# The first layer of the compression MLP, moved from small fp32 products to the unit ring, with the token windows stationary

## The reference, cut to what matters

```python
def _compress(z, pe, w1, w2):          # z: (B, T, G, D), T = 256, G = 2; D = 192 for keys, 128 for values
    ch = z.reshape(B, T // CMP_STRIDE, CMP_STRIDE, G, D)          # stride 16, block 32 tokens
    nc = T // CMP_STRIDE - r + 1                                  # 15 blocks
    blk = jnp.concatenate([ch[:, i:i + nc] for i in range(r)], axis=2)
    blk = blk + pe[None, None, :, None, :]
    flat = blk.transpose(0, 1, 3, 2, 4).reshape(B, nc, G, CMP_BLOCK * D)
    return jax.nn.silu(flat @ w1) @ w2                            # w1: (32 * D, 256)
```

## Time and profile before

| | before |
|---|---|
| median of three executions | 2555.05 us |
| the profiled execution, its own time | 2549.53 us |
| its span, first to last instruction | 2547.3 us |
| mean granted TensorE clock | 0.986 |
| TensorE busy | 2486.6 us (98%) |
| TensorE weight loads busy | 2435.2 us (96%) |
| VectorE busy | 1444.2 us (57%) |
| ScalarE busy | 1162.5 us (46%) |
| GpSimd busy | 125.4 us (5%) |
| HBM read | 408.33 MB, 161 GB/s over the span |

### The profile page before, as it was taken

The page is one execution under the profiler, slowest core; times in us unless marked ns, Lnnn a source line. Parts: engine busy times, 40 slices in busy tenths (PEclk is TensorE's granted clock), DMA queues, the critical chain, the costliest instruction groups (busy, mean ns, idle before and its releaser), DMA issues.

```text
span 2547.3 us, 51023 instructions
## 1 busy us (share of the span) xinstructions
PE 2486.6 (98%) x19836; PEld 2435.2 (96%) x19836; DVE 1444.2 (57%) x2171; ACT 1162.5 (46%) x1645; POOL 125.4 (5%) x161
## 2 busy tenths in 40 slices
PE   7999999999999999999999999999998989999987
PEld 7999999899999999999999999999998979999987
DVE  6666335765565555455554556555555456755645
ACT  5555224443454444434443445554454445655542
POOL 3000210000001000000000001000000100000001
PEclk9999989999999999999999999999999989999999
DMA  6446664446666666666676657646554635645543
GB/s 251 164 164 163 181 164 112 117 133 182 178 184 183 182 182 189 190 182 181 182 197 180 183 163 212 169 136 164 139 162 109 166 100 150 166 132 145 152 132 99
DMA packets 750335, 415.20 MB, mean 163 GB/s; under 512 B 44432, under 2 KB 738704, under 8 KB 750224
## 3 DMA queue, kind: packets, MB, share of 16 engines
q1 hardware_dynamic: 746448, 400.78, 56.3%
q0 software_dynamic: 2944, 10.49, 1.3%
q10 hardware_dynamic: 832, 2.36, 0.2%
HBM read 408.33 MB, written 2.10 MB: 161 GB/s over the span
## 4 chain that ended last, share of the span: by engine, by line
PE 90%; DVE 4%; ACT 2%; issue 2%; DMA 1%; POOL 0%; ACTq 0%; DVEq 0%; SPq 0%; POOLq 0%
PE ps_unit L248 26%; PE ps_unit L250 26%; PE ps_unit L249 26%; DVE w_lo L235 1%; PE ps_score L565 1%; ACT w_hi L228 1%; PE ps_score L988 1%; POOL work L2479 0%; PE ps_out L833 0%; PE ps_norm L833 0%; DVE work L351 0%; DVE work L2410 0%; PE ps_score L812 0%; PE ps_norm L1344 0%; PE ps_turn L812 0%
## 5 line engine op out<-in xcount | busy, mean ns | idle before, releaser
L235 DVE TENSOR_TENSOR w_lo<-raw,w_hi 128x1024 fp32r<-128x1024 f32 (+1 forms) x756 | 885.6, 1213 | 242.1 <-ACT w_hi L228 241.2
L228 ACT ACTIVATE w_hi<-raw 128x1024 fp32r<-128x1024 f32 (+1 forms) x756 | 764.1, 1042 | 420.8 <-PE ps_unit L250 418.8
L248 PE MATMUL ps_unit<-b_hi,w_hi 128*128 128x256 f32 (+1 forms) x3184 | 911.2, 286 | 6.0 <-DVE w_lo L235 6.0
L250 PE MATMUL ps_unit<-b_hi,w_lo 128*128 128x256 f32 (+1 forms) x3184 | 906.1, 285 | 0.0
L249 PE MATMUL ps_unit<-b_lo,w_hi 128*128 128x256 f32 (+1 forms) x3184 | 904.4, 284 | 0.0
L248 PE MATMUL ps_unit<-a_hi,w_hi 128*128 128x256 f32 (+1 forms) x2768 | 795.3, 287 | 5.3 <-DVE w_lo L235 3.1
L249 PE MATMUL ps_unit<-a_lo,w_hi 128*128 128x256 f32 (+1 forms) x2768 | 787.5, 284 | 0.0
L250 PE MATMUL ps_unit<-a_hi,w_lo 128*128 128x256 f32 (+1 forms) x2768 | 787.2, 284 | 0.0
L248 PEld LDWEIGHTS ps_unit<-b_hi,w_hi 128*128 128x128 f32 x3184 | 602.0, 189 | 11.9 <-issue 5.1
L250 PEld LDWEIGHTS ps_unit<-b_hi,w_lo 128*128 128x128 f32 x3184 | 602.5, 189 | 0.0
L249 PEld LDWEIGHTS ps_unit<-b_lo,w_hi 128*128 128x128 f32 x3184 | 599.8, 188 | 0.7
(11 more groups left out here) (368 smaller groups left out, 1723.7 us busy)
## 6 DMA issues: line engine op xcount, KB each, us to landing
raw<-in_attn_w_in SPq DMA_DIRECT2D x96, 512.0 KB, 4.9
raw<-in_gla_w_in SPq DMA_DIRECT2D x96, 512.0 KB, 4.4
raw<-in_w_in SPq DMA_DIRECT2D x88, 512.0 KB, 4.8
raw<-in_w_ffn_gate SPq DMA_DIRECT2D x88, 512.0 KB, 4.6
raw<-in_w_ffn_up SPq DMA_DIRECT2D x88, 512.0 KB, 4.7
raw<-in_w_fox SPq DMA_DIRECT2D x64, 512.0 KB, 4.1
raw<-in_w_ffn_down SPq DMA_DIRECT2D x64, 512.0 KB, 4.7
raw<-in_w_out SPq DMA_DIRECT2D x32, 512.0 KB, 4.5
```

Of the source, the lines that this page charges most:

```text
L228: act.activation(hi[:, b % 4, 0:size], raw[:, b % 8, 0:size], ACT.Copy)\
L235: dve.tensor_tensor(lo[:, b % 4, 0:size], raw[:, b % 8, 0:size], hi[:, b % 4, 0:size], ALU.subtract).then_inc(lo_ready, 1)
L248: pe.matmul(dst, wh, xh[:, k0 + k, 0:N], start=start and k == 0, stop=False)
L250: mm = pe.matmul(dst, wl, xh[:, k0 + k, 0:N], start=False, stop=stop and k == kb - 1)
```

## The change

The first layer's operands change sides and its weights enter the ring. The 80 tiles of w1 (32 of 128 key rows, 16 that hold the 64 tail rows of two neighbouring positions one above the other, 32 of values) are laid out on the host as `w_cmp`, 20 blocks of four 128x256 tiles, in the order `CMP_ORDER`. Ten new units `cmp_unit` of two such blocks stand behind slots 5 to 14; they pass raw, `w_hi` and `w_lo` like all others. The windows are split too, into 30 high and 30 low columns side by side (`window_hi` on ScalarE, `window_lo` on VectorE, in slots 3, 4 and 9), and stand stationary, up to 128 columns of them (60 of the tile, and the next tile's first). Each tile takes two products of 256 moving columns, one with `w_hi` and one with `w_lo`, into PSUM rows 0 to 59 of `psS[1]`, where the rows of high and low windows stay apart. At U_NQ ScalarE copies the 60x512 result (`chs`), and four fp32 products with the constant K_SUM add the two halves and turn it; one Silu of 128x120 follows. The tails' windows are now made by VectorE in eight small instructions (`cmp_tails`), for which slot 2's evacuation is written twice. GpSimd's weight loads and its tail windows are gone.

```diff
-U_NQ = U_NKV + 15
+U_NQ = U_NKV + 25
+CMP_ORDER = [*range(32), *range(33, 48), 32, 48, *range(50, 80), 49]
...
+        def cmp_tails(dve):
+            dve.wait_ge(evacuated, nkv(2) + 1)
...
+                        ins = dve.tensor_tensor(cpt[p, 8 * half:8 * half + 8, g * NB_C:(g + 1) * NB_C],
+                                                win, pe_b, ALU.add)
+            ins.then_inc(cp_tails, 1)
...
+        def window_hi(act, m):
+            act.wait_ge(*((cp_ready, 1), (cp_tails, 1), (cp_ready, 2))[m])
+            act.activation(window(0, m), cw[m][0], ACT.Copy).then_inc(cw_hi, 1)
+        def window_lo(dve, m):
+            dve.wait_ge(cw_hi, m + 1)
+            dve.tensor_tensor(window(1, m), cw[m][0], window(0, m), ALU.subtract).then_inc(cw_lo, 1)
+        def cmp_unit(pe, c):
+            U = nkv(5 + c) + 1
+            for h in range(2):
+                b = 2 * U + h
+                pe.wait_ge(lo_ready, b + 1)
+                for t in range(4):
...
+                    rows = min(P, 60 * (n - j))
+                    dst = psS[1][0:rows, T * (m == 2):T * (m == 2) + T]
+                    x = x[:, 60 * j:60 * j + rows]
+                    pe.matmul(dst, x, hi[:, b % 4, T * t:T * (t + 1)], start=q in (0, 48), stop=False)
+                    mm = pe.matmul(dst, x, lo[:, b % 4, T * t:T * (t + 1)], start=False, stop=q in (47, 79))
+                mm.then_inc(block_done, 1)
-        def cmp_piece(pe, m):
...
-            for jj in range(4):
-                for h in range(2):
-                    mm = pe.matmul(cmp_banks[2 * (src == 2) + h][:, 0:30],
-                                   w1s[0:p, m % 3, jj, h * P:(h + 1) * P], x[0:p, j + jj, :],
...
                     if slot in (9, 10, 14):
-                        nsa_turn_v(pe, (9, 10, 14).index(slot), U - 1)
-                    if slot >= 4:
-                        for _ in range(2):
...
-            for m in pieces:
-                cmp_piece(pe, m)
+                        nsa_turn_v(pe, (9, 10, 14).index(slot), nkv(slot - 1))
+                    if slot >= 5:
+                        cmp_unit(pe, slot - 5)
...
+                    pe.wait_ge(cm_h, 1)
+                    for m in range(4):
+                        mm = pe.matmul(psS[0][:, 30 * m:30 * m + 30], chs[:, P * m:P * m + P],
+                                       con[0:60, K_SUM:K_SUM + 30], start=True, stop=True)
...
-                    for v in range(2):
-                        for h in range(2):
-                            ins = act.activation(hsl[:, v, h, :], cmp_banks[2 * v + h][:, 0:30], ACT.Silu)
+                    act.wait_ge(cm_t, 1)
+                    ins = act.activation(hsl.rearrange("p v h n -> p (v h n)"), psS[0][:, 0:120], ACT.Silu)
...
-            for m in range(3, len(CPIECES)):
-                cmp_load(pool, m)
```

More of the change, by code:

```diff
@@ L521, in program @@
         nk_vt, nk_v = sem("nk_vt"), sem("nk_v")
-        cw_full = [sem(f"cw_full{n}") for n in range(3)]
-        cw_used, cp_ready = sem("cw_used"), sem("cp_ready")
+        cp_ready, cp_tails, cw_hi, cw_lo = (sem("cp_ready"), sem("cp_tails"), sem("cw_hi"), sem("cw_lo"))
+        cm_sum, cm_h, cm_t = sem("cm_sum"), sem("cm_h"), sem("cm_t")
         cm_hs, cm_kc, cm_kcr, cm_sq, cm_ms, cm_rs = (
@@ L526, in program @@
         w2_full = sem("w2_full")
[L529 to L543, removed]
+        w_cmp = a["w_cmp"]
@@ new lines, in nkv @@
+        def nkv(slot):
+            return U_NKV + slot + max(0, slot - 5)
+        def cmp_tails(dve):
+            dve.wait_ge(evacuated, nkv(2) + 1)
+            for x in range(2):
+                p = slice(64 * x, 64 * x + 64)
+                for g in range(NSA_G):
+                    for half in range(2):
+                        win = kt2[p, g, 16 * half:16 * half + 240]\
+                            .rearrange("p (n m x) -> p m n x", m=8, x=2)[:, :, :, x]
+                        pe_b = VB[p, V_PET + 8 * half:V_PET + 8 * half + 8].unsqueeze(2)\
+                            .broadcast_to([64, 8, NB_C])
+                        ins = dve.tensor_tensor(cpt[p, 8 * half:8 * half + 8, g * NB_C:(g + 1) * NB_C],
+                                                win, pe_b, ALU.add)
+            ins.then_inc(cp_tails, 1)
@@ L1746, in _ @@
                 fox(h)
[L1747 to L1754, removed]
+            for slot in range(15):
+                U, st = nkv(slot), slot // 5
+                ck, cv = ((C_KC, C_VC), (C_KS, C_VS), (C_KW, C_VW))[st]
+                if slot % 5 == 2:
+                    load_tails(sp, U, 0, 0, ck)
+                else:
+                    load_unit(sp, U, 0, 0, w_in, (ck, ck + NSA_DK, 0, cv, cv + P)[slot % 5])
+                if slot >= 5:
+                    for h in range(2):
+                        load_block(sp, U + 1, h, 0, 0, w_cmp[2 * (slot - 5) + h]
+                                   .rearrange("p (k m) -> p k m", m=P))
             with sp.Fori(0, 4) as i:
@@ L1845, in _ @@
                 fox(h)
-            pieces = iter(range(len(CPIECES)))
             for st in range(3):
                 for s in range(5):
-                    U, slot = U_NKV + 5 * st + s, 5 * st + s
+                    slot = 5 * st + s
+                    U = nkv(slot)
                     mm_unit(pe, U, 0, 0, AH, AL)
@@ L2057, in _ @@
             for slot in range(15):
[L2058 to L2059 removed]
+                U = nkv(slot)
+                if slot >= 5:
+                    split_hi(act, U + 1, 0, 0)
+                split_hi(act, nkv(slot + 1), 0, 0, tails=1 if slot in (1, 6, 11) else None)
                 if slot == 0:
@@ L2065, in _ @@
                     fox_out_hi(act, FOX_H - 1)
+                if slot == 9:
+                    act.wait_ge(block_done, 2 * U)
+                if slot in (3, 4, 9):
+                    window_hi(act, (3, 4, 9).index(slot))
                 if slot in (7, 12):
@@ L2081, in pair @@
                 n = 0 if first else 2 * (i - 1)
+                if first:
+                    act.wait_ge(block_done, 2 * U_NQ)
+                    act.activation(chs, psS[1][0:60, :], ACT.Copy).then_inc(cm_h, 1)
                 split_hi(act, U_NQ + 1, 4, i)
@@ L2091, in pair @@
                     nsa_exp(act, n)
-                split_hi(act, U_NQ + 2, 4, i, tails=i + 1)
+                split_hi(act, U_NQ + 2, 4, i, tails=i + 2)
                 if first:
@@ L2267, in _ @@
             for slot in range(15):
-                U, g, k = U_NKV + slot, slot % 5, slot // 5
-                split_lo(dve, U + 1, 0, 0)
+                U, g, k = nkv(slot), slot % 5, slot // 5
+                nxt, more = nkv(slot + 1), 1 + (slot >= 5)
+                if slot >= 5:
+                    split_lo(dve, U + 1, 0, 0)
+                    lo_block(dve, 2 * nxt)
+                else:
+                    split_lo(dve, nxt, 0, 0)
                 if slot == 1:
```

80 lines of the change are left out of this document (46 added, 34 removed).

## The result

| | before | after |
|---|---|---|
| median | 2555.72 us (4 executions, 2552.21 to 2556.85) | 2509.19 us (4 executions, 2506.33 to 2512.49) |
| the profiled execution, its own time | 2549.53 us | 2511.03 us |
| its span | 2547.3 us | 2509.2 us |
| mean granted TensorE clock | 0.986 | 0.992 |

The ratio of the changed kernel's time to the other's is 0.9828, 95% interval 0.9812 to 0.9843: 1.7% faster, 46.5 us by the medians. The forecast was 2514.5 us with a range of 2507 to 2532.

What follows compares the result with a forecast made beforehand. TensorE, busy 98% of the span, was taken to bound the kernel. Terms -46.9 - 14.1 + 19.1 + 0.9 + 0.5 = -40.5 us took 2555.05 to 2514.5 us, range 2507 to 2532.

Steps and rivals of the forecast that it cites:

- The old products, 46.9 us: Eleven groups of 30-column fp32 products on TensorE, 0.22 us a product, would go: 46.9 us removed.
- The clock, 14.1 us: Eleven units between and behind the old products would return to 5.72 us each at full clock: 14.1 us removed.
- The new products, 0.119 us each, 19.1 us: 160 fp32r products of 256 columns on TensorE, in ten new units, priced like existing units' products: 19.1 us added.
- The fp32-price rival: New products' window loads cost 0.22 us each, 35 us instead of 19, giving 2530.5 us; chance 0.06.
- The last rival: A small product costs by moving columns: old ones worth 5 us, the change adds 20, giving 2570 us; chance 0.01.
- The four small products, 0.9 us: Four fp32 products of 30 columns at U_NQ, 0.22 us each: 0.9 us added on TensorE.
- VectorE late behind slots 8 and 13, 0.5 us: Behind the norms there, the next unit waits for VectorE's evacuation of the shared PSUM bank, twice 0.3: 0.5 us added.
- Loading, ScalarE, GpSimd at nothing: In the shortened stage, SP's loads at 237 GB/s, ScalarE at 50 of 88 us and GpSimd's work add no time.
- The starving ring: w1's loads on SP's queue come too slowly, a slot takes 12.65 us, giving 2565 us; chance 0.02.
- The rival of the low clock: TensorE's clock stays down for another reason, such as heavy loading: +21 us, giving 2535 us; chance 0.06.
- The stage: From the end of slot 4's unit to the end of U_NQ's: 88 us forecast, against 128.63 before.
- The step that was off: The 40.5 us saving, derived from a profiled execution of 2549.5 us, was subtracted from the median of 2555.05 us.

Runs made afterwards that it cites:

- wide: The kernel before with each small product's 30 moving columns repeated eight times, 240 in all, same weight loads; 2570.61 us.
- same sides: The changed kernel with w1's split blocks stationary again and 60 or 30 window columns moving, in fp32r, first layer's result not formed; 2538.49 us.
- rows512: The changed kernel with w1's blocks laid out so that each load is made of 512 B rows instead of 4 KB ones; 2509.74 us.
- the other comparison: The kernel before and the changed kernel, both unedited, timed again with more rounds: medians 2553.85 and 2508.71 us, ratio 0.9827.
- few old: The kernel before with 52 of its 192 small products left, loads and order kept, most of the first layer's sum left out; 2521.63 us.
- dve_plus1: The changed kernel with one more VectorE instruction of 128x1024 behind the fourth split of each of slots 5 to 14; 2508.72 us.
- dve_plus2: The changed kernel with two more VectorE instructions of 128x1024 in each of slots 5 to 14; 2515.46 us.

## Why the prediction was right, and where it was off

- **The old products, 46.9 us**: right for the profiled execution. In the longer course the groups take 49.4 and 50.5 us, since they run partly at the low clock too ("the groups themselves hardly slow" did not hold there).
- **The clock, 14.1 us**: the mechanism was right and shown from two sides (wide and same sides). The size was that of one of two courses; in the other the stage is 7.1 us longer.
- **The new products, 0.119 us each, 19.1 us**: measured 0.1175, and 19.6 us for the ten groups with the slower first product behind each norm or transpose. The fp32-price rival (stationary cuts at every 60th column) is out. The last rival, by which a small product costs by its moving columns, is out as well, and same sides shows it on its own ground: 30 and 60 columns cost the same 0.11 us. The table for products by themselves in the Trainium skill's page "TensorE: Matmul & The Clock Gate", section "Back-to-back issue gap", gives no price for this stream, and what the section says of streams, that loads and products both set the spacing, is what the trace agrees with.
- **The four small products, 0.9 us**: 1.01 us.
- **VectorE late behind slots 8 and 13, 0.5 us**: 0.2 us at slot 10's unit, none at U_NQ. The walk was right in kind: the row of instructions without a gap ends at 303.18.
- **Loading, ScalarE, GpSimd at nothing**: right. 255 GB/s with a share of 0.94, against 237 estimated, and no wait of TensorE for a load. The estimate was low because the stage moves 22.1 MB now, not "the same bytes", 20.8. The starving ring is out, and rows512 shows that there is room.
- **The rival of the low clock**, 21 us, is out: the clock is 1.00 in the whole stage. Its 1.6 us a unit are the loss of one slow unit (7.3 - 5.7); by the mean over the eleven in the earlier trace rows, 7.00 - 5.72 = 1.28, it would have cost some 17 us and stood at the edge of the range, not outside it.
- **The stage**: 88 us forecast (87.2 by the prediction's own terms), 86.66 measured, against a profile it was to be 41.4 us shorter without the four products, and was 42.0.
- **The step that was off** is the last: "It is 5.5 under the median, which is what is predicted: 2555.05 - 40.5". It carried the saving of an execution of the shorter course over to a median that stands near the longer one: three of the four executions behind the 2555.72 us took 2555.05 to 2556.85, as the two profiled ones of the longer course did (2555.61 and 2556.56). In the other comparison, of nine, the median was 2553.85. The 5.5 us between the profiled execution and the median, noted in the prediction, were largely this stage, which differs by 7.1 us between the courses, and so part of what the change could remove. With the longer course the sum would have been -47.6 us and the forecast 2507.4, with both equally often 2511.0; measured were 2509.2. It wasn't cancelling errors that kept the forecast near: each of its five terms stands within 1 us of what the first profiles before and after show.

Outside the stage the spans differ by little: 2417.5 to 2418.8 us in the four profiles before, 2418.4 and 2422.5 in the two after, of which 1.0 are the four products. The rest appears without the change too: wide and few old, both made from the kernel before, stand at 2421.0 and 2422.6. One piece of it shows in all three long ones, at the first hand-over to the second block's attention. TensorE idles there in every kernel, and the granted clock of the 20 us around it is 1.00 in the first profile before and the second after, and 0.83 in the first profile after and in wide and few old. Why it falls in some executions isn't settled.

No experiment with the whole computation in it was faster than the changed kernel: dve_plus1's 2508.72 us and rows512's 2509.74 are single times inside its 2506.33 to 2512.49.

## What to carry to other kernels

A product with few moving columns was paid twice here: by its 128 stationary columns, and by the clock of whatever stood behind it. When one operand is thin (here 30 rows against 256), make the thin one stationary and stream the wide one. A gap of several us between the profiled execution and the median can be a part of the kernel that runs in more than one way: look for it in several profiles before a saving is carried from one to the other, above all where the granted clock is under 1.00. And before taking work from the bounding engine, ask what that work covers: here the next 13.6 us would have brought 3.5.

## What the runs showed of the hardware that I had not expected

- The clock loss behind small products made the same kernel's stage 128.5 to 128.6 us long in two profiled executions and 135.7 to 135.8 in two others, with nothing between in these four.
- A TensorE kept busy without a gap was granted 0.65 of the clock in a unit behind small products; its busy time alone does not show it.
- A record of a plain fp32 product with 240 moving columns takes 0.197 us, one of fp32r with 256 takes 0.1175. At 30 columns both types cost 0.109 to 0.111.
- VectorE was busy for 89.03 of 90.19 us in dve_plus2, and the stage was only 3.5 us longer for it.
